# Four load buffers and three v parts in the expert stage, and filler matmuls divided evenly over attention's units

## The reference, cut to what matters

```python
s = neighbourhood_scores(q, k) * scale + bias          # 8 heads
p = softmax(s); na_o = p @ v
...
q = (ht @ w_q).reshape(T, 8, 2, 128)
s = einsum('thpd,hpnd->thpn', q, sub_keys)             # two lists of 128 keys
experts, gates = best 16 of the 16 x 16 sums of the best 16 of each list
ue, ve = u[experts], v[experts]                        # 8 x 16 rows of 1024 per token
a = gelu(einsum('td,tkd->tk', xt, ue))
out = einsum('tk,tkd->td', gates * a, ve)
```

## Time and profile before

| | us |
|---|---|
| median of three runs (2600.38, 2618.66, 2600.66) | 2600.66 |
| the profiled execution | 2617.26 |
| its span, first to last instruction | 2615.5 |
| TensorE busy | 2427.2 |
| VectorE busy | 1826.7 |
| GpSimd busy | 1314.5 |
| ACT busy | 937.1 |

### The profile page before, as it was taken

The page is one execution under the profiler, slowest core; times in us unless marked ns, Lnnn a source line. Parts: engine busy times, 40 slices in busy tenths (PEclk is TensorE's granted clock), DMA queues, the critical chain, the costliest instruction groups (busy, mean ns, idle before and its releaser), DMA issues.

```text
span 2615.5 us, 34593 instructions
## 1 busy us (share of the span) xinstructions
PE 2427.2 (93%) x12777; PEld 2045.1 (78%) x12777; DVE 1826.7 (70%) x3571; ACT 937.1 (36%) x1426; POOL 1314.5 (50%) x892
## 2 busy tenths in 40 slices
PE   7979999999989998999999998998998989888887
PEld 7769999999866766888888887886877767666766
DVE  4773894454387797668984694984875777777776
ACT  4443544654333223333333332332332333233333
POOL 0000895000566754634444575785883765666640
PEclk9987999999988899999999999999999999999999
DMA  5433667666666646744444579779677888888885
GB/s 168 157 127 137 206 221 244 231 219 224 234 190 199 225 147 227 256 147 143 145 143 140 206 255 345 245 254 377 214 245 276 300 294 303 286 293 305 300 303 194
DMA packets 252679, 596.84 MB, mean 228 GB/s; under 512 B 35792, under 2 KB 118224, under 8 KB 251872
## 3 DMA queue, kind: packets, MB, share of 16 engines
q1 hardware_dynamic: 182496, 385.69, 42.9%
q0 software_dynamic: 67712, 201.61, 22.9%
q10 hardware_dynamic: 2304, 7.34, 0.8%
HBM read 521.12 MB, written 73.40 MB: 227 GB/s over the span
## 4 chain that ended last, share of the span: by engine, by line
PE 29%; DMA 19%; POOL 6%; DVE 5%; SPq 4%; issue 2%; ACT 2%; DVEq 0%; ACTq 0%
PE ps L793 23%; DMA g_in<-gates 14%; PE ps L823 3%; POOL a_got L471 3%; POOL picked L466 3%; DMA act_in<-acts 2%; DMA raw<-in_experts 2%; PE ps L1039 2%; SPq L378 1%; SPq L375 1%; SPq L356 1%; DMA picked<-in_experts,vidx 1%; DVE acc_odd L1521 1%; DVE v_lo L1559 1%; DVE acc L1521 1%
## 5 line engine op out<-in xcount | busy, mean ns | idle before, releaser
L466 POOL DMA_INDIRECT picked<-in_experts,vidx x384 | 542.9, 1414 | 656.9 <-PE ps L793 220.2
L793 PE MATMUL ps<-ht_hi,sp_hi 128*128 128x256 f32 (+1 forms) x2048 | 703.5, 344 | 18.8 <-DVE sp_lo L1568 14.5
L793 PE MATMUL ps<-ht_lo,sp_hi 128*128 128x256 f32 (+1 forms) x2048 | 692.0, 338 | 0.0
L793 PE MATMUL ps<-ht_hi,sp_lo 128*128 128x256 f32 (+1 forms) x2048 | 691.8, 338 | 0.0
L471 POOL DMA_INDIRECT a_got<-acts,aidx x384 | 470.7, 1226 | 127.8 <-issue 116.1
L462 POOL TENSOR_TENSOR sp_lo<-raw,sp_hi 128x1024 fp32r<-128x1024 f32 x112 | 297.5, 2670 | 454.0 <-ACT sp_hi L682 453.9
L793 PEld LDWEIGHTS ps<-ht_hi,sp_hi 128*128 128x128 f32 x2048 | 391.4, 191 | 63.9 <-DVE sp_lo L1568 19.7
L793 PEld LDWEIGHTS ps<-ht_hi,sp_lo 128*128 128x128 f32 x2048 | 390.4, 191 | 41.0
L793 PEld LDWEIGHTS ps<-ht_lo,sp_hi 128*128 128x128 f32 x2048 | 391.2, 191 | 36.5
L793 PE MATMUL ps<-v_hi,w_hi 128*128 128x512 f32 x768 | 308.6, 402 | 66.1 <-DVE w_lo L1553 60.4
L1568 DVE TENSOR_TENSOR sp_lo<-raw,sp_hi 128x1024 fp32r<-128x1024 f32 x144 | 176.4, 1225 | 225.4 <-ACT sp_hi L682 225.2
(11 more groups left out here) (187 smaller groups left out, 3634.1 us busy)
## 6 DMA issues: line engine op xcount, KB each, us to landing
raw<-in_experts SPq DMA_DIRECT2D x256, 512.0 KB, 3.7
v_raw<-in_experts SPq DMA_DIRECT2D x128, 512.0 KB, 3.6
raw<-in_front SPq DMA_DIRECT2D x104, 512.0 KB, 3.3
acts<-act_g SPq DMA_DIRECT2D x128, 256.0 KB, 3.3
act_in<-acts SPq DMA_DIRECT2D x128, 192.0 KB
acts<-act_g SPq DMA_DIRECT2D x128, 128.0 KB, 2.1
gates<-stage SPq DMA_DIRECT2D x16, 1024.0 KB, 11.6
g_in<-gates SPq DMA_DIRECT2D x128, 128.0 KB
```

Source lines behind the costliest of these rows:

```text
L466: pool.indirect_dma_start(picked[n % SLOTS][:, :], None, v_rows, bass.IndirectOffsetOnAxis(ap=vidx[:, n // P, n % P:n % P + 1], axis=0)).t ...
L793: last = pe.matmul(out, l, r, start=start and k == 0, stop=stop and k == 2, skip_group_check=True)
```

## The change

It has two parts.

The V stage: the loaded buffers v_raw, act_in and g_in exist four times (RING) instead of twice, with a semaphore for each; v_hi and v_lo exist three times. SyncE loads steps 2 and 3 as soon as the U stage is done, and in its loop step r + 4 where it loaded r + 2; x2d and fgain go out at r = 2. ACT and VectorE make v_hi and v_lo of r + 2 where they made those of r + 1. The third v_hi lies where act_g lay, and waits for the last store of activations; the third v_lo waits for the end of the U stage. w_f, w_hi and w_lo still exist twice.

Attention: `na_part` gives every unit 24 / (tiles) matmuls, 12 for q = 0 and 6 for q = 1, and TensorE issues them between the transposes and the product, no longer behind the product. A chunk begins with each head's first unit.

```diff
-        v_raw = sb("v_raw", A0 + 32 * KB, [P, 2, 1024])
-        v_hi = sb("v_hi", A0, [P, 2, 1024], F32R)
-        v_lo = sb("v_lo", A0 + 8 * KB, [P, 2, 1024], F32R)
-        act_in = sb("act_in", A0 + 21 * KB, [P, 2, HALF])
-        g_in = sb("g_in", A0 + 52 * KB, [P, 2, 2 * P])
+        v_raw = sb("v_raw", A0 + 32 * KB, [P, RING, 1024])
+        v_hi = [sb(f"v_hi{k}", A0 + at * KB, [P, 1024], F32R) for k, at in enumerate((0, 4, 48))]
+        v_lo = [sb(f"v_lo{k}", A0 + at * KB, [P, 1024], F32R) for k, at in enumerate((8, 12, 60))]
+        act_in = [sb(f"act_in{k}", A0 + at * 512, [P, HALF]) for k, at in enumerate((42, 45, 112, 115))]
+        g_in = sb("g_in", A0 + 52 * KB, [P, RING, 2 * P])
...
-        def na_parts(q, n):
-            units = NA_HEADS * TILES[q]
-            return range(24 * n // units, 24 * (n + 1) // units) if n < units else range(0)
+        def na_part(q, n):
+            per = TILES[q]
+            return (n // per, 24 // per * (n % per), 24 // per * (n % per + 1)) if n < NA_HEADS * per else None
...
             for r in range(N_KEYS):
                 if r == 0:
                     sp.wait_ge(S["a_done"], STEPS)
+                    for k in range(2, RING):
+                        load_v(k)
+                        load_weights(k)
+                if r == 2:
                     sp.dma_start(x2d[:, :, :], a["x2_park"][:, SPARSE:, :]).then_inc(S["x2_in"], 16)
                     sp.dma_start(fgain[:, :], a["fgain"].partition_broadcast(P)).then_inc(S["fg_in"], 16)
...
-                if r + 2 < N_KEYS:
+                if r + RING < N_KEYS:
                     sp.wait_ge(S["v_lo"], r + 1)
-                    load_v(r + 2)
+                    load_v(r + RING)
                     sp.wait_ge(S["w_ready"], r + 1)
-                    load_weights(r + 2)
+                    load_weights(r + RING)
...
             def v_part(r):
-                act.wait_ge(v_in[r % 2], 16 * (r // 2 + 1))
-                if r >= 2:
-                    act.wait_ge(S["y_done"], r - 1)
-                act.activation(v_hi[:, r % 2], v_raw[:, r % 2], ACT.Copy).then_inc(S["v_hi"], 1)
+                act.wait_ge(v_in[r % RING], 16 * (r // RING + 1))
+                if r == 2:
+                    act.wait_ge(act_out[1], 8 * STEPS)
+                if r >= 3:
+                    act.wait_ge(S["y_done"], r - 2)
+                act.activation(v_hi[r % 3][:, :], v_raw[:, r % RING], ACT.Copy).then_inc(S["v_hi"], 1)
...
+            v_part(1)
             for r in range(N_KEYS):
                 act.wait_ge(S["w_ready"], r + 1)
                 if r >= 2:
                     act.wait_ge(S["y_done"], r - 1)
                 act.activation(w_hi[:, r % 2], w_f[:, r % 2], ACT.Copy).then_inc(S["w_hi_ready"], 1)
-                if r + 1 < N_KEYS:
-                    v_part(r + 1)
+                if r + 2 < N_KEYS:
+                    v_part(r + 2)
...
                         last.then_inc(S["na_turned"], 1)
+                    part = na_part(q, n)
+                    if part:
+                        t_part(q, C_RET_QK + part[0], part[1], part[2])
                     if n >= 3:
...
                         last.then_inc(S["na_summed"], 1)
-                    for p in na_parts(q, n):
-                        t_part(q, C_RET_QK + p // 3, p % 3)
...
             v_part(0)
             weights(0)
+            v_part(1)
             for r in range(N_KEYS):
                 weights_lo(r)
                 if r + 1 < N_KEYS:
                     weights(r + 1)
                 visits(r >= 8)
-                if r + 1 < N_KEYS:
-                    v_part(r + 1)
+                if r + 2 < N_KEYS:
+                    v_part(r + 2)
                 visits(8 <= r and r % 8 == 0 and done < VISITS - 8)
```

More of the change, by code:

```diff
@@ L220, in encoder_program @@
         u_in = [S[f"u_in{i}"] for i in range(RING)]
-        v_in, gate_in = ([S[f"{n}{i}"] for i in range(2)] for n in ("v_in", "g_in"))
-        act_out, act_in_done = ([S[f"{n}{i}"] for i in range(2)] for n in ("act_out", "act_in"))
+        v_in, gate_in, act_in_done = ([S[f"{n}{i}"] for i in range(RING)] for n in ("v_in", "g_in", "act_in"))
+        act_out = [S["act_out0"], S["act_out1"]]
         acc_in = [S[f"acc_in{t}"] for t in range(SPARSE)]
@@ L374, in load_v @@
             def load_v(r):
-                sp.dma_start(v_raw[:, r % 2, :], a["experts"][r, 1]).then_inc(v_in[r % 2], 16)
+                sp.dma_start(v_raw[:, r % RING, :], a["experts"][r, 1]).then_inc(v_in[r % RING], 16)
             def load_weights(r):
-                sp.dma_start(act_in[:, r % 2, :], acts_rows[1][r, :, P:]).then_inc(act_in_done[r % 2], 16)
-                sp.dma_start(g_in[:, r % 2, :], a["gates"][r, :, SPARSE * P:(NT - 1) * P]).then_inc(gate_in[r % 2], 16)
+                sp.dma_start(act_in[r % RING][:, :], acts_rows[1][r, :, P:]).then_inc(act_in_done[r % RING], 16)
+                sp.dma_start(g_in[:, r % RING, :], a["gates"][r, :, SPARSE * P:(NT - 1) * P]
+                             ).then_inc(gate_in[r % RING], 16)
             load_x(0)
@@ L818, in t_part @@
                         pe.wait_ge(S["gelu_done"], N_KEYS - 1 + n)
-                for e in range(8 * part, 8 * part + 8):
+                for e in range(first, end):
                     k, which = e // 3, e % 3
@@ L859, in t_chunk @@
             def t_chunk(q, c):
-                for part in range(3):
-                    t_part(q, c, part)
+                t_part(q, c, 0, 24)
             def v_chunk(q, c):
@@ L1061, in add_experts @@
                         cols = slice(c * 512, c * 512 + 512)
-                        last = exact(ps[:, 2 + 2 * d + c, :], w, (v_hi[:, par, cols], v_lo[:, par, cols]),
+                        last = exact(ps[:, 2 + 2 * d + c, :], w, (v_hi[r % 3][:, cols], v_lo[r % 3][:, cols]),
                                      r == 0, r == N_KEYS - 1)
@@ L1246, in front @@
                         add_mask(q, n // nt + 1)
-                    for c in na_begins(q, n - 1):
+                    c = na_begins(q, n - 1)
+                    if c is not None:
                         lo(q, C_RET_QK + c + AHEAD)
@@ L1545, in weights @@
                     dve.wait_ge(S["w_lo_ready"], r - 1)
-                dve.tensor_tensor(w_f[:, r % 2, 2 * P:], act_in[:, r % 2, 2 * P:], stage[:, r, :], ALU.mult)
-                dve.tensor_tensor(w_f[:, r % 2, 0:2 * P], act_in[:, r % 2, 0:2 * P], g_in[:, r % 2], ALU.mult
+                dve.tensor_tensor(w_f[:, r % 2, 2 * P:], act_in[r % RING][:, 2 * P:], stage[:, r, :], ALU.mult)
+                dve.tensor_tensor(w_f[:, r % 2, 0:2 * P], act_in[r % RING][:, 0:2 * P], g_in[:, r % RING], ALU.mult
                                   ).then_inc(S["w_ready"], 1)
@@ L1558, in v_part @@
                 dve.wait_ge(S["v_hi"], r + 1)
-                dve.tensor_tensor(v_lo[:, r % 2], v_raw[:, r % 2], v_hi[:, r % 2].bitcast(F32), ALU.subtract
+                if r == 2:
+                    dve.wait_ge(S["a_done"], STEPS)
+                dve.tensor_tensor(v_lo[r % 3][:, :], v_raw[:, r % RING], v_hi[r % 3][:, :].bitcast(F32), ALU.subtract
                                   ).then_inc(S["v_lo"], 1)
```

24 lines of the change are left out of this document (14 added, 10 removed).

## The result

The changed kernel takes 2522.3 us (median of four runs, 2510.8 to 2525.4) where the kernel before took 2604.8 beside it: a ratio of 0.9665, 95% interval 0.9635 to 0.9695, so 3.1 to 3.7% faster. The forecast was 2528 us, in a range from 2500 to 2568. The profiled execution took 2519.6 us (span 2517.8).

What follows compares the result with a forecast made beforehand. It took the V stage to be held by load latency in two-buffer rings, 4.79 us a step against TensorE's 4.08. Gains of 59 + 5 + 8 + 1 = 73 us off 2600.7 gave 2528 us, range 2500 to 2568.

Steps and rivals of the forecast that it cites:

- The number of a step: V stage: the stretch at 2032.33 us begins with r = 8, giving 110 steps of 4.79 us each.
- The steps with visits: V stage, r = 8 to 117: rings of four cut steps from 4.79 to 4.25 us, gaining 59 us (34 to 78).
- TensorE and DMA tie at 4.1 us: V stage: two tied servers don't both run full, so a step takes 4.25 us, between 4.08 and 4.48.
- a loop of latency: V stage: with two buffers, loads taking 4.76 us must land within about one step, losing 0.71 us per step.
- rival 2: V stage gains nothing because SyncE issues in order: 2587 us; chance 0.09 together with Rival 3 short of its point.
- The third pair of parts at no cost: V stage: ACT making v_hi two steps ahead adds no new wait in the steady state, cost nothing.
- The beginning: Start of the V stage: earlier loads of steps 2 to 5 gain 5 us, between 2 and 7.
- Attention of the second sequence: Four-tile attention: six fillers per unit ahead of the product gain 8 of 12.2 us; 12 at best, 3 lost at worst.
- Attention of the first sequence: Two-tile attention: fillers of 12 and 12 instead of 8 and 16 gain 1 us, at most 4.
- Carried over to the median: Whole kernel: the 73 us saving worked out on the profiled execution applies unchanged to the median run of 2600.7 us.
- Rival 1: V stage: DMA share does not pass 0.92, 4.48 us a step, gain 48 us, 2553 us; chance 0.22.
- Rival 3: V stage: GpSimd's gathers become the bound, 2630 us from a mean of 2.0 us on; chance past that point 0.04.

Runs made afterwards that it cites:

- e10: Changed kernel plus one 192 KB load in each V stage step that nothing reads, against the kernel before: 2533.0 us, ratio 0.9713.
- e8: Kernel before with only SyncE's order changed, the factors' loads issued ahead of the load of v: 2553.0 us, ratio 0.9798.
- e3: Changed kernel with four load buffers but two buffers per split part, split one step ahead; against the kernel before: 2532.5 us, ratio 0.9732.
- e5: Changed kernel with the evenly divided filler matmuls put back behind each product; against the kernel before: 2520.5 us, ratio 0.9676.
- e6: Changed kernel with fillers in the old lumps of eight, in front of the product; against the kernel before: 2525.5 us, ratio 0.9695.
- e9: Changed kernel with VectorE's visits ahead of the chunk split in the second attention; against the kernel before: 2518.6 us, ratio 0.9653.
- e11: Repetition of the unaltered changed kernel, timed against the kernel before: 2527.0 us, ratio 0.9676.
- e7: Changed kernel with the third tile's activation gathers replaced by a constant, half the V stage's gathers; against the kernel before: 2522.1 us, ratio 0.9683.

## Why the prediction was right

The stage, the wait and the size of the whole were read rightly. The cause of the wait, the number of one step and the reason for attention's gain were not.

*The number of a step.* The prediction says that the stretch at 2032.33 us begins with r = 8. It begins with r = 9; r = 8 had begun at 2027.94, which is the very 2027.9 that the prediction works out as the time without a loss. So the 4.5 us that it saw lost before r = 8 were step r = 8 itself, and the step in the middle took 4.83 us, not 4.79. That the slip does no harm to the sum is luck: with the right number the steps would have been given 110 x (4.83 - 4.25) = 64 us and the beginning 0.5, together what 59 + 5 gave.

*The steps with visits.* Forecast 4.25 us and 59 us of gain; measured 4.18 us and 531.7 - 459.5 = 72 us. Of the 13 us between, 5 are the step's number, 8 the 4.18. The limits that were worked out hold: TensorE's 4.08 us is reached to within 0.1 us, and the stage's 348 to 354 GB/s against the 387 of e10 put the DMA's own limit at no more than 4.18 x 351 / 387 = 3.79 us, where 3.81 had been worked out. The 8 us were lost at the step "TensorE and DMA tie at 4.1 us. Two servers that tie don't both run full": they did not tie, since a DMA busy share of one was no full server. The row with queued DMAs had said so; it was taken for a bound, and the middle was then priced by the share.

*"The ring has two buffers ... a loop of latency."* The loop was there, but not for want of buffers. SyncE's factors' loads stood behind the wait for v_lo(r), the last thing that VectorE does in a step, although they needed only w_f(r), done earlier in it; e8 takes that away and 80% of the stage's gain follows. The prediction saw the order of issue (its rival 2 rests on it) and asked whether it would spoil the ring, not whether it was the fault to begin with. Rings, third part and the later x2d and fgain together are worth the other 15 us.

*The third pair of parts at no cost.* Right, and it is also worth little: 3.5 us of stage, where e3 leaves it out.

*The beginning.* Forecast 5 us, between 2 and 7; 37.8 to 35.7 us from r = 0 to r = 8, so 2.0. The sign "r = 8 within 37 us of r = 0" came, but the kernel before missed it by only 0.8 us. What there was to gain was the idle time ahead of r = 2: r = 1 took 6.8 us and takes 4.2, while r = 0 takes 0.6 us longer, the lateness that was allowed for. ACT's v_hi(2) still waits for its load (at 1971.86, 5.26 us), now without two megabytes ahead of it.

*Attention of the second sequence.* Forecast 8 us, measured 10 in the stretch. VectorE's waits for scores are 2.7 us, as said (under 5); that one stands at the first score, ahead of the window of rows 15, so all of the 12.2 us went, where 8 had been taken. The reason given was wrong in half: the product's place was argued at length and shortens nothing (e5, e6). The clock was to be 0.95 and was 0.91, and VectorE's mix did meet the later product, 4.0 us, the loss that the lower bound held. That the wait for sp_hi stays was right: 15.3 us in eight waits from 714 to 874 us (the ninth of the 18.2 lies ahead), and e9 shows what it was worth.

*Attention of the first sequence.* Forecast 1 us. VectorE's waits for scores fell from 4.0 to 2.0 us, and the waits for the product rose from 0.6 to 5.8 us (both 69 to 115 us), as the lower bound had it. The last product starts at 115.6 us instead of 117.5, and the first key score at 264.9 us instead of 265.4: some 0.5 us are left.

*Carried over to the median.* 73 us forecast, 2604.8 - 2522.3 = 82.5 measured, 97.7 between the two profiled executions. The stages that the change touches hold 74.3 + 10.2 = 84.5 of it; 8 us lie in the second U stage (837.5 to 829.5), which e11 does not repeat.

*Rivals.* Rival 1 (the DMA keeps the stage) had the largest chance and falls by e10. Rival 2 (the stage gains nothing) falls by the steps of 4.18 us. Rival 3 (GpSimd) did not reach its point: 1.53 us per gather, where 2.0 was the point and 1.83 the straight line. The line was drawn too low, since the seven gathers of its row are cut by the window's edges: the whole ones took 3.66 and 2.52 us, 3.09 in the mean, and the line through that gives 2.0. The rise is thus further from straight than the prediction thought. The rule of the Trainium skill (GPSIMD Engine Reference, Specifications), that GpSimd's SBUF interfaces contend with VectorE instructions with two SBUF inputs, is not tested by e7, where VectorE is as busy (172.55 against 171.03 of 200 us, the same instructions). e7 shows that something else counts too: a gather of v takes 1.11 us instead of 1.48 when those of the activations are not between them. Why, no run shows.

## What to carry to other kernels

Where an engine issues several loads in order, each behind a wait of its own, ask first for which of them the wait ahead is not its own: here exchanging two waits gave 80% of what two more buffers and a third part gave, and it cost no memory. What the issuing engine itself waited for (SPq above) tells of it in one line. An entry in the chain, a busy share near one, or 200 us of waits on an engine with slack is no price; a run that halves the suspect's work, or adds to it, gives the price (here 5 and 7 us). In a pipeline of small units like this attention, spread the filler work evenly, and give the engine that sets the pace its independent work ahead of the instruction that waits, not behind it.

## What was not expected of the hardware

The mean busy share of the DMA engines reads 0.98 at 348 GB/s and 1.04 at 387 GB/s in the same loop: near one it says little of what is left; the landing of a v_raw load, 3.7 us before, is 5.9 us in the changed kernel and 9.5 with the additional load, and the steps hardly change, since the ring hides it.

A gather of 128 rows of v takes GpSimd 1.48 us with one of the activations between each two, and 1.11 us without, with VectorE equally busy.

TensorE's granted clock over the second attention, a mean over stretches at 1.2 and at 2.4 GHz, rose with each step that shortened the gaps between its matmuls, for the same 640 of them: 0.83 with uneven fillers, 0.92 with even ones (e5), 0.99 with the visits ahead; TensorE's busy time fell with it from 150.8 to 140.2 and 130.0 us. Whether the clock gave part of the time or only followed the shorter gaps was not separated.
